# Fetching the sample's value pages by indirect gather in a hybrid RWKV-7 / forgetting-attention decoder step

## The reference

```python
past_k = cache_k[l][page_table].reshape(n_seq, n_pages * PAGE_SIZE, B_HEADS, B_HEAD_DIM)
past_v = cache_v[l][page_table].reshape(n_seq, n_pages * PAGE_SIZE, B_HEADS, B_HEAD_DIM)
...
s_past = (jnp.einsum('bqhd,bkhd->bhqk', q, past_k).astype(jnp.float32) * scale
          + F_new[..., None] - F_past)
...
p = jax.nn.softmax(jnp.concatenate([s_past, s_new], axis=-1), axis=-1)
o = (jnp.einsum('bhqk,bkhd->bqhd', p[..., :p_len].astype(past_v.dtype), past_v)
     + jnp.einsum('bhqk,bkhd->bqhd', p[..., p_len:].astype(v.dtype), v))
```

## Time and profile before

| | |
|---|---|
| time, median of 3 executions | 2503.57 us |
| lowest, highest | 2499.07, 2526.43 us |
| span of the profiled execution | 2497.7 us |
| PE busy | 2028.1 us (81%) |
| DVE busy | 1670.3 us (67%) |
| POOL busy | 1433.6 us (57%) |
| stretch of value page products | 515.1 to about 875 us |
| PEER gathers (LATE) | from 926.8 us to the end |

### The profile page before, as it was taken

The page is one execution under the profiler, slowest core; times in us unless marked ns, Lnnn a source line. Parts: engine busy times, 40 slices in busy tenths (PEclk is TensorE's granted clock), DMA queues, the critical chain, the costliest instruction groups (busy, mean ns, idle before and its releaser), DMA issues.

```text
span 2497.7 us, 32001 instructions
## 1 busy us (share of the span) xinstructions
PE 2028.1 (81%) x10334; PEld 838.4 (34%) x10334; DVE 1670.3 (67%) x3942; ACT 292.5 (12%) x641; POOL 1433.6 (57%) x1559
## 2 busy tenths in 40 slices
PE   5999999888889977878887778996766766767675
PEld 4444454533446666423232123331111111111111
DVE  3888898864544458667666866656878877667642
ACT  2112222331112111111000101010000000000000
POOL 0332232233333315777777777777876777777774
PEclk9999999899999999999999999998999999999998
DMA  8776776597576739999999999999999999999997
GB/s 304 266 250 217 221 252 203 190 356 235 179 266 222 233 105 354 397 382 403 400 389 334 394 387 367 403 387 373 364 361 336 371 347 360 377 369 357 375 365 272
DMA packets 264363, 794.63 MB, mean 318 GB/s; under 512 B 33296, under 2 KB 64756, under 8 KB 263576
## 3 DMA queue, kind: packets, MB, share of 16 engines
q0 software_dynamic: 191008, 680.63, 74.0%
q1 hardware_dynamic: 73216, 112.20, 12.9%
HBM read 781.60 MB, written 11.11 MB: 317 GB/s over the span
## 4 chain that ended last, share of the span: by engine, by line
POOL 40%; PE 26%; issue 18%; DVE 6%; DMA 4%; POOLq 2%; another core or an unknown queue 1%; ACT 1%; PEld 0%; SPq 0%; PEldq 0%; DVEq 0%; ACTq 0%
POOL arena L982 40%; PE bank L1007 11%; PE bank L1158 2%; PE bank L1163 2%; PE bank L1296 2%; POOLq L959 2%; DMA arena<-in_w_ada 1%; PE bank L1425 1%; DVE arena L2832 1%; DMA arena<-in_peer_v,arena 1%; PE bank L1149 1%; PE bank L1150 1%; PE bank L1100 1%; PE bank L1013 1%
## 5 line engine op out<-in xcount | busy, mean ns | idle before, releaser
L1628 PE MATMUL bank<-arena 128*32 128x512 f32 x2048 | 933.2, 621 | 338.3 <-DMA arena<-in_peer_v,arena 290.2
L2832 DVE CUSTOM_DVE_ANT_0 arena<-arena 128x1024 f32<-128x1024 f32 x512 | 624.2, 1221 | 344.6 <-DMA arena<-in_peer_u,arena 305.6
L982 POOL DMA_INDIRECT arena<-in_peer_u,arena x520 | 581.7, 1119 | 242.5 <-issue 155.1
L982 POOL DMA_INDIRECT arena<-in_peer_v,arena x520 | 575.0, 1106 | 206.4 <-issue 153.1
L1628 PEld LDWEIGHTS bank<-arena 128*32 128x32 f32 x2048 | 180.9, 111 | 1006.0 <-DMA arena<-in_peer_v,arena 536.5
L1007 PE MATMUL bank<-arena 128*128 128x128 f32 (+6 forms) x1512 | 374.7, 403 | 7.6 <-DVE arena L2173 2.7
L964 POOL DMA_DIRECT2D arena<-in_cache_k x256 | 137.4, 537 | 327.9 <-issue 210.7
L1696 ACT ACTIVATE arena<-bank 128x512 f32<-128x512 f32 (+11 forms) x354 | 150.9, 426 | 1259.0 <-PE bank L1659 220.5
L964 POOL DMA_DIRECT2D arena<-in_cache_v x256 | 137.3, 536 | 260.6 <-issue 154.8
L1007 PEld LDWEIGHTS bank<-arena 128*128 128x128 f32 (+2 forms) x1512 | 232.6, 188 | 150.6 <-issue 137.6
L2109 DVE TENSOR_TENSOR arena<-arena 128x512 f32<-128x512 f32 x256 | 175.4, 686 | 33.6 <-DMA arena<-scratch_queries 17.1
(11 more groups left out here) (298 smaller groups left out, 1609.1 us busy)
## 6 DMA issues: line engine op xcount, KB each, us to landing
arena<-in_cache_k POOLq DMA_DIRECT2D x256, 256.0 KB, 3.7
arena<-in_cache_v POOLq DMA_DIRECT2D x256, 256.0 KB, 4.1
arena<-in_w_ada SPq DMA_DIRECT2D x12, 2048.0 KB, 13.1
arena<-in_w_in SPq DMA_DIRECT2D x10, 2048.0 KB, 10.2
arena<-in_peer_wq SPq DMA_DIRECT2D x16, 1024.0 KB
arena<-in_peer_u,arena POOLq DMA_INDIRECT x520
arena<-in_peer_v,arena POOLq DMA_INDIRECT x520
scratch_gates<-arena SPq DMA_DIRECT2D x16, 256.0 KB, 2.7
```

What stands on the lines that cost most here:

```text
L982: nc.gpsimd.indirect_dma_start(gathered[:, j, :], None, tables[kind[0]][:, :], OFF(ap=index, axis=0)).then_inc(row_in[j], 16)
L1628: ins = mm(acc[u][32 * j:32 * (j + 1), :], spread[:, n % 2, b, :], gathered_row(("v", t, x))[:, 512 * u:512 * (u + 1)], start=x < 4, stop= ...
L2832: release(nc.vector.tensor_tensor_reduce(out=row, in0=row, in1=h2[:, t, :], scale=1.0, scalar=0.0, op0=MUL, op1=ADD, accum_out=gelu[:, at: ...
```

## The change

Key pages are fetched as before. Value pages are fetched by indirect gathers: one for each page, 128 rows of 2 KB, row numbers taken from a column of `key_row` in SBUF, which has all 256 pages' row numbers, one partition a token. To make them, SP broadcasts the page table to 128 partitions, a third load counted in `ids_in`, and DVE turns it into `page * 128 + partition` with three instructions on [128 x 256]. POOL's loops for the values become 256 written-out gathers, each behind its own wait for the slot. `ids_row` lives shorter, a constant column is added, and the slots, PE's order and DVE's other work stay.

```diff
-    ("ids_row", NS * PAGES, LOAD, CHAIN), ...
+    ("ids_row", NS * PAGES, LOAD, FOX), ("key_row", NS * PAGES, LOAD, CHAIN), ...
...
             load(buf("ids_row")[0:1, :].bitcast(I32), page_table.rearrange("(o b) g -> o (b g)", o=1), ids_in)
+            load(buf("key_row").bitcast(I32), page_table.rearrange("(o b) g -> o (b g)", o=1).to_broadcast([P, NS * PAGES]), ids_in)
...
-            pool.wait_ge(ids_in, 32)
+            pool.wait_ge(ids_in, 48)
...
-            for past, cache in enumerate((cache_k, cache_v)):
-                rows_of = cache.rearrange("l n s h d -> (l n) s (h d)")
...
+            rows_of = cache_k.rearrange("l n s h d -> (l n) s (h d)")
...
+            past_values = cache_v.rearrange("l n s h d -> (l n s) (h d)")
+            pool.wait_ge(key_rows_ready, 1)
+            for k in range(NS * PAGES):
+                j = k % RING
+                pool.wait_ge(page_free[j], NS * PAGES // RING + k // RING + 1)
+                nc.gpsimd.indirect_dma_start(pages[:, j, :], None, past_values[:, :],
+                                             OFF(ap=buf("key_row")[:, k:k + 1].bitcast(U32), axis=0)).then_inc(page_loaded[j], 16)
...
             link(nc.vector.tensor_copy(tot[:, 0:16], prefix[:, :, P - 1]), signal=prefix_ready, at=1)
+            dve.wait_ge(ids_in, 48)
+            key_row = buf("key_row")
+            link(nc.vector.tensor_copy(key_row, key_row.bitcast(I32)))
+            link(stt(key_row, key_row, float(PAGE), const("place_of").to_broadcast([P, NS * PAGES]), MUL, ADD))
+            link(nc.vector.tensor_copy(key_row.bitcast(U32), key_row), signal=key_rows_ready, at=1)
```

More of the change, by code:

```diff
@@ L52 @@
 _at = 0
-for _name, _n in [("ident", P), ("ones", P), ("rows", (NS + 1) * P), ("iota", TOP), ("eye", NS * NS), ("fold", H), ("headones", P),
+for _name, _n in [("ident", P), ("ones", P), ("rows", (NS + 1) * P), ("iota", TOP), ("place_of", 1), ("eye", NS * NS), ("fold", H), ("headones", P),
                   ("causal", P), ("suffix", P),
@@ L84, in constants @@
     put("ident", np.eye(P))
+    put("place_of", p[:, None] * 1.0)
     put("headones", (p[:, None] // HD == p[None, :] // HD) * 1.0)
@@ L210 @@
     ("rows", ROW_RING * D, LATE, LATE), ("spread", 2 * TOP * 32, LATE, LATE), ("pick_i", 2 * P, OUT, LATE), ("idx_t", 2 * P, LATE, LATE),
-    ("ids_row", NS * PAGES, LOAD, CHAIN), ("ids_col", 2, LOAD, LOAD), ("svalue", 32, PRE, CHAIN),
+    ("ids_row", NS * PAGES, LOAD, FOX), ("key_row", NS * PAGES, LOAD, CHAIN), ("ids_col", 2, LOAD, LOAD), ("svalue", 32, PRE, CHAIN),
     ("so_col", 32, CHAIN, CHAIN), ("idx_f", SLOTS, OUT, LATE), ("idx_s", NS, LATE, LATE),
@@ L525, in hybrid_step @@
         ids_in, forget_in, logf_in = sem("ids_in"), sem("forget_in"), sem("logf_in")
+        key_rows_ready = sem("key_rows_ready")
         w_in_slot = [sem("w_in_slot0"), sem("w_in_slot1")]
@@ L953, in _ @@
             ids = buf("ids_row")[0:1, :].bitcast(I32)
-            for past, cache in enumerate((cache_k, cache_v)):
-                rows_of = cache.rearrange("l n s h d -> (l n) s (h d)")
[L956 to L965, removed]
+            rows_of = cache_k.rearrange("l n s h d -> (l n) s (h d)")
+            with pool.Fori(0, NS) as b:
+                with pool.Fori(0, PAGES // RING) as g:
+                    for half in range(0, RING, 4):
+                        four = [pool.value_load(ids[:, ds(b * PAGES + g * RING + half + i, 1)], min_val=0, max_val=POOL - 1)
+                                for i in range(4)]
+                        for j, page in enumerate(four, half):
+                            pool.wait_ge(page_free[j], b * 4 + g + 1)
+                            pool.dma_start(pages[:, j, :], rows_of[ds(page, 1), :, :].rearrange("o p d -> (o p) d"))\
+                                .then_inc(page_loaded[j], 16)
+            past_values = cache_v.rearrange("l n s h d -> (l n s) (h d)")
[5 more added lines that the diff above has]
+                                             OFF(ap=buf("key_row")[:, k:k + 1].bitcast(U32), axis=0)).then_inc(page_loaded[j], 16)
             tables = {"u": peer_u.rearrange("l e d -> (l e) d"), "v": peer_v.rearrange("l e d -> (l e) d")}
```

## The result

| | kernel before | changed kernel | ratio, 95% interval |
|---|---|---|---|
| median | 2507.95 us (4 runs) | 2633.93 us (4 runs) | 1.0484 [1.0434, 1.0534] |
| lowest, highest | 2499.07, 2526.43 | 2631.99, 2639.43 | |

The changed kernel is slower by 126 us; I had said 30, and the range ended at 2546. In each of the six jobs all kernels were of one kind. I call them the 2510 and the 2455 kind of job, after the kernel before. The result above is of the 2510 kind, and so was the profile on which I predicted.

What follows compares the result with a forecast made beforehand. PE was taken to bound the kernel, with POOL's page supply almost equal to its pace. Terms 12 + 8 + 9 + 1 = +30 us on the profiled 2497.7 us gave 2527.7, forecast as 2531 us with 3.7 for timed executions; range 2508 to 2546.

Steps and rivals of the forecast that it cites:

- PE's own pace is 1.26 us a page: From 600 to 877 us, PE takes four pages in 5.04 us, almost equal to POOL's supply of 1.30 us a page.
- Number 4: Rival: stalls fall where PE waits most, and a gather holds DVE in turn; +50 us, 2554 us; 5%.
- PRE: Phase from 515 to 600 us: gathers of pages 8 to 63 stalled by DVE's eleven two-input passes, +12 us.
- CHAIN and pauses: 600 to 877 us: 192 pages at 1.34 against 1.30 us, +8; three pauses where the old loop hid a reading, +9.
- start: Kernel's beginning: one more SP load and DVE's three instructions for row numbers, +1 us, bounds 0 and 2.
- A plain DMA of 0.536 us becomes a gather: Value page fetches on POOL: each gather takes 0.94 us plus 0.30 to the next, 1.24 us a page undisturbed.
- Rival 2: Gather cost follows bytes, not rows: about 0.47 us each, supply faster than PE; -40 us, 2464 us; 5%.
- Gathers are stalled by DVE: A gather issued during DVE's two-input pass waits for its end, then needs 0.82 us; stall is the pass's rest less 0.12.
- Rival 1: DVE passes do not stall gathers, which run at 1.24 us a page; -5 us, 2499 us; 12%.
- rival 3: Gathers stalled, but part of PE's new waits is covered by waits it had anyway; +15 us, 2516 us; 12%.
- DVE's wait at PRE's end: At about 600 us, DVE's wait for PE grows from 23.9 to about 36 us.
- From the last page's issue to the end, unchanged at 1628.6: Stretch behind the last value page's issue keeps its length, near 1628.6 us.

Runs made afterwards that it cites:

- e14: Key pages gathered, value pages fetched by register read and plain DMA, against the kernel before: 2623.6 us, 1.043 (2510 kind).
- e12: Changed kernel, but each value page fetched by a register read and plain DMA, written out, against the kernel before: 2502.8 us, 0.998 (2510 kind).
- e9: The changed kernel a third time, against the kernel before: 2636.9 us, 1.049 (2510 kind).
- e1: Changed kernel's start and layout, but the old loop of plain DMAs for value pages, against the kernel before: 2455.4 us, 1.001 (2455 kind).
- e2: Changed kernel, but each value page fetched by a register read and plain DMA, written out, against the kernel before: 2444.2 us, 0.997 (2455 kind).
- e5: The changed kernel once more, in another job, against the kernel before: 2481.6 us, 1.010 (2455 kind).
- e11: Changed kernel with DVE's two-input passes of 2.3 us in the 515 to 600 us phase cut into quarters, against the kernel before: 2627.9 us, 1.045 (2510 kind).
- e13: Every second value page gathered, the others by register read and plain DMA, against the kernel before: 2500.0 us, 0.994 (2510 kind).
- e15: Small unused gathers after every second key page, key page numbers fixed, value pages by read and plain DMA, against the kernel before: 2543.5 us, 1.010 (2510 kind).
- e18: Changed kernel with an unused register read ahead of each gather, against the kernel before: 2492.9 us, 1.018 (2455 kind).

## Why the prediction was wrong

**What failed is the step "PE's own pace is 1.26 us a page"**, kept fixed beside gathers. I gave every cost of a gather to POOL, asked only when the page would come, and put what gathers do to PE at nothing, without a reason. In the kind of job that both profiles are of, a row of gathers also holds back PE's reports to ACT, DVE and POOL (6.1 us at 929, up to 5.1 us for pages) and, in e14, PE's own instructions. The stretches of the result against before: up to page 8 +4.2 us, pages 8 to 63 +25.2 (96.0 for 70.8), pages 63 to 255 +95.1 (376.6 for 281.4), behind it +10.6; together 135, the difference of the two spans. None of the rivals had this. Number 4 had its sign, but 50 us, and its cause was stalls and a DVE that gathers hold. That gathers are what costs is shown, by e12 beside e9; how they reach PE is not.

**The rest of the sum stood**, as the 2455 kind shows, where nothing holds PE. The two kernels of the table come from different jobs of that kind, and kernels of one kind differ by some us in such stretches (63 to the last: 280.0 in e1, 281.1 in e2), so that agreement to 1 or 2 us is in part luck:

| term | predicted | changed kernel there (e5) against plain DMAs (e1) |
|---|---|---|
| PRE | +12 | pages 8 to 63: 84.1 for 69.9 us, +14.2 |
| CHAIN and pauses | +17 | page 63 to the last: 297.9 for 280.0 us, +17.9 |
| start | +1 | no difference (e1: 1.001) |
| last page issued near | 898 | 900.3 |
| time | +30 | +25 (1.010 [1.007, 1.014]) |

- *A plain DMA of 0.536 us becomes a gather*: 0.94 least, 1.05 mean; I had said 0.94 and near 1.1. Rival 2, half the cost for half the bytes, is excluded.
- *Gathers are stalled by DVE*: shown, and by e11 that it is the rest of the pass. In the 2455 kind the gather at 530.81 took 1.92 us and ended 0.82 us after DVE's pass of 529.56 to 531.91; all eighteen of its page gathers of over 1.4 us end so, 0.82 or 0.83 us after a two-input pass. The stall in PRE is 66.3 - 56 x 0.945 = 13.4 us (predicted 14.7). Rival 1 is excluded, and rival 3, +15 us, lies just under the +16 to +33 of the interval in the 2455 kind.
- *CHAIN* and *the pauses* were taken at +8 and +9; only their sum is measured.
- *DVE's wait at PRE's end* was to grow from 23.9 to 36: it is 30.3 in the 2455 kind, 29.4 in the result, half of the growth.
- *From the last page's issue to the end, unchanged at 1628.6*: 1639.2. In the 2510 kind it was 1628.6 to 1641.5 in all kernels, 1573.5 to 1587.7 in the other.

**It stood in the profile before, in a stretch that I had read for prices only.** The products of PEER's stage from 1000 us on, which run beside 1040 gathers in rows: first the kernel before of the profile I had, then e1, the same work in the 2455 kind (busy us, mean ns, idle before and its releasers):

```profile
L1628 PE MATMUL bank<-arena 128*32 128x512 f32 x2032 | 927.5, 621 | 337.0 <-DMA arena<-in_peer_v,arena 288.9 <-issue 44.0 <-ACT arena L1696 3.4
...
L982 POOL DMA_INDIRECT arena<-in_peer_v,arena x514 | 566.7, 1103 | 201.1 <-issue 151.6 <-remote 49.2 <-PE bank L1628 0.3
```

```profile
L1632 PE MATMUL bank<-arena 128*32 128x512 f32 x2048 | 939.9, 612 | 292.7 <-DMA arena<-in_peer_v,arena 291.7 <-issue 0.2
...
L986 POOL DMA_INDIRECT arena<-in_peer_v,arena x516 | 563.7, 1093 | 166.2 <-issue 152.4 <-PE bank L1632 13.9
```

44.0 us of PE by issue, where the other kind has 0.2, and 49.2 us of POOL on "remote", in the one stage that gathers in rows; up to 900 us there is no "remote". It is the mark of the kind: from 1060 us to the end this group's idle time by issue is 34.8 to 69.1 us in all nine traces of the 2510 kind and 0.2 us in all eleven of the 2455 kind, and POOL's "remote" is 33 us or more in the nine and absent from the eleven. It costs little there, since that stage waits for DMA anyway: the stretch behind the last value page is 41 us longer in the kernel before of the first profile than in e1, most of what separates a kernel before of 2508 us from one of 2456. I took the gathers' length from these rows and did not ask what their neighbours did meanwhile. CHAIN, in which PE is busy 90% and PE, ACT and DVE wait for each other, pays 95 us for 192 gathers.

**The clock** is part of the size, how large a part is open. At 0.83 the 1920 small products of line 1435 take 91.7 us of PE instead of 69.4, and its idle time by issue around them comes on top. The late reports are not the clock's doing: of the 248 page reports that the result's trace has, 26 come 2.4 to 5.1 us after the start of the page's last product, and 22 of these products began where the clock was granted in full. In the kernel before the longest is 1.2 us.

## What to carry to other kernels

Before an instruction is moved into a busy stage, look at a stage that already has it in rows and read not its length but its neighbours: idle time by issue and "remote" waits there, and nowhere else, are its price to others. The same gathers, 0.94 us of POOL each, were free where only every second page was gathered (0.996 and 0.994, so 0.4 and 0.6% under the kernel before in the two kinds of job) and cost 1.0 or 4.9% in rows. Alternating gathers with plain DMAs also hides each read of a page number behind a gather. And when a measured loss is several times what the sum says, run the pair again in another job before looking for the missing term.

## What the runs showed of the hardware that was not expected

- In three of the six jobs, rows of gathers on GpSimd (0.94 us each, 0.30 between) held TensorE's semaphore reports (a product that ended at 929.2 us was reported at 935.38) and its instructions (e14); in the other three they did not, in any of eleven traces. The changed kernel itself ran in two jobs of the first kind and one of the other. What sets the kind is open. It is not the kernel, and not the number of the chip: e5 and e13 ran on the same one.
- The Trainium skill's page "SBUF — State Buffer", section "SBUF: two separate sides", says that PE never waits on another's port. No run here contradicts that for ports; but PE beside rows of gathers went from 40 matmuls in 1.56 us to one in 2.8 us (e14), so that GpSimd's gathers are not free of cost to PE. The path is not shown: e15 was to tell the gather's instruction from its transfer and did not.
- A gather that DVE's pass stalls gets in between two passes 0.034 us apart, and ends 0.82 us after the first of them (e11, eighteen of eighteen).
- A register read costs POOL 0.61 us between two plain DMAs (e12) and nothing beside a gather (e13, e18).
